# FFN down projection with two levels of seven products, the weight sums made by accumulating DMAs

## What is computed

```
h = _rmsnorm(x, norm_ffn_g[l]) * (1.0 + sc2) + sh2
y = (jax.nn.silu(h @ w_gate[l]) * (h @ w_up[l])) @ w_down[l]
x = x + g2 * y
...
return _rmsnorm(x, final_norm_g)
```

## Time and profile before

| | us |
|---|---|
| median of 3 runs | 3537.9 |
| lowest and highest | 3532.1, 3541.24 |
| span of the profiled execution (first to last instruction) | 3532.7 |
| PE busy in it | 3365.4 (95%) |
| DVE busy in it | 1703.2 (48%) |
| last product of the up projection ends | 3260.4 |
| passes 2, 4, 1, 3, 5, 7 of the down projection (L3409) | 226.6 |
| pass 6 (L3415) | 37.8 |
| from its end to the end of the span | 7.9 |

### The profile page before, as it was taken

How to read it: one execution, slowest core, us unless ns; L and a number is a source line. 1 busy time by engine, 2 the same in 40 slices (tenths; PEclk the granted TensorE clock), 3 DMA queues, 4 the chain that set the end, 5 groups by cost and what they waited for, 6 DMA issues and landing times. The chain is left out here.

```text
span 3532.7 us, 43811 instructions
## 1 busy us (share of the span) xinstructions
PE 3365.4 (95%) x17353; PEld 1781.7 (50%) x17353; DVE 1703.2 (48%) x2971; ACT 887.7 (25%) x1814; POOL 441.8 (13%) x329
## 2 busy tenths in 40 slices
PE   7999999899999899999979999898999999999999
PEld 4544444566555544444454577556654444444443
DVE  3579999766556400000124356555643434434336
ACT  2321111455332212111132122223543111111001
POOL 0033451222000011111201111111000000000000
PEclk8999999999999799999989999999999999999999
DMA  5213231222555699999952132213030111111434
GB/s 191 84 56 129 96 114 61 95 71 39 176 197 213 228 378 405 405 407 404 331 198 74 63 119 67 92 55 109 22 107 19 36 48 48 36 48 51 144 109 167
DMA packets 209426, 502.72 MB, mean 142 GB/s; under 512 B 22572, under 2 KB 93431, under 8 KB 195674
## 3 DMA queue, kind: packets, MB, share of 16 engines
q1 hardware_dynamic: 193090, 462.49, 35.9%
q0 software_dynamic: 10416, 30.14, 3.1%
q10 hardware_dynamic: 5736, 7.53, 0.6%
HBM read 447.90 MB, written 57.21 MB: 143 GB/s over the span
## 5 line engine op out<-in xcount | busy, mean ns | idle before, releaser
L600 PE MATMUL ch_side<-aT,space 128*128 128x512 f32 x896 | 393.2, 597 | 0.0
L1938 PE MATMUL jn_duo<-space,dsa 128*128 128x512 f32 (+1 forms) x736 | 328.4, 599 | 3.5 <-ACT dsa L2021 3.1
L600 PEld LDWEIGHTS ch_side<-aT,space 128*128 128x128 f32 x896 | 168.7, 191 | 213.0 <-issue 211.0
L3301 PE MATMUL en_bank<-en_h,en_up 128*128 128x512 f32 x528 | 233.8, 592 | 0.0
L1938 PEld LDWEIGHTS jn_duo<-space,dsa 128*128 128x128 f32 (+1 forms) x736 | 124.3, 173 | 151.6 <-issue 151.6
L2058 DVE TENSOR_TENSOR dsa<-dsa,jn_duo 128x512 f32<-128x512 f32 x24 | 16.5, 687 | 335.2 <-PE jn_duo L1938 335.2
L726 DVE MAX8 ch_best<-ch_score 128x8 f32<-128x384 f32 (+5 forms) x192 | 171.6, 894 | 6.1
L2452 PE MATMUL mx_duo<-mx_chunks,mx_region 128*128 128x512 f32 x384 | 172.3, 603 | 0.0
L727 DVE MATCH_REPLACE8 ch_score<-ch_best,ch_score 128x384 f32<-128x384 f32 (+5 forms) x192 | 168.0, 875 | 0.0
L3301 PEld LDWEIGHTS en_bank<-en_h,en_up 128*128 128x128 f32 x528 | 100.2, 190 | 125.8 <-issue 125.8
L3301 PE MATMUL en_bank<-en_h,en_mixed_up 128*128 128x512 f32 x352 | 158.2, 592 | 0.0
(11 more groups left out here) (596 smaller groups left out, 5643.9 us busy)
## 6 DMA issues: line engine op xcount, KB each, us to landing
space<-exp_w SPq DMA_DIRECT2D x62, 2048.0 KB, 21.6
aT<-exp_w SPq DMA_DIRECT2D x34, 2048.0 KB, 20.2
en_up<-w_down SPq DMA_DIRECT2D x132, 256.0 KB, 3.6
space<-ada_w SPq DMA_DIRECT2D x12, 2048.0 KB, 8.6
space<-w_ada SPq DMA_DIRECT2D x12, 2048.0 KB, 8.4
space<-proj_padded SPq DMA_DIRECT2D x96, 256.0 KB, 3.6
aT<-w_in SPq DMA_DIRECT2D x7, 2048.0 KB, 8.6
en_up<-w_gate SPq DMA_DIRECT2D x22, 512.0 KB, 4.6
```

The costliest lines, as they stand in the source:

```text
L600: last = nc.tensor.matmul(side_ps[i % 2][:, :], hT[:, k, t * P:(t + 1) * P], w[n % 2][:, k, :], start=k == 0, stop=k == KD - 1)
L1938: last = nc.tensor.matmul(ps[mine, :], xT[:, k, mine], up_view(ring[place])[:, k, :], start=k == 0, stop=k == KD - 1)
L3301: last = nc.tensor.matmul(to[:, :], a[:, k, :], b[:, k, :], start=k == 0, stop=k == HK - 1)
```

## The change

The down projection is cut a second time. FINE = 4, 1, 2, 5, 7, 6 are the six outer products that come first; each is now made by seven inner products again, on halves of 256 columns and 256 tokens. LAST = 3 is made as pass 6 was before, tile by tile.

- A fine step takes two slices of A and two of w_down (STARTS = 0, 2, 5, 7, 9; five steps) and makes the seven inner products, each of two matmuls of 128 tokens by 256 columns: 14 matmuls (L3446). Slice 4 is left over (ODD): `odd_step` does it plainly in eight matmuls of 256 columns. All eight banks are in use in every pass.
- `split` on DVE makes the inner sums for a fine step: two additions of 128x512 and four of 128x256, on A and on the weights in turn, two steps ahead of PE. `mix_act` sums the outer blocks of A in place, two slices at once. After each pass `post` adds the inner products into the four corners of the outer product (eight additions from PSUM) and ACT copies the first; `collect` and `settle` put the outer products together.
- The outer sums of w_down are no longer made on DVE. SP loads the first block of a sum into a ring of eight places of two slices (512 KB), and POOL issues DMAs that add the other blocks to it in memory (`accum_op`, L3597). TERMS gives the blocks: four for product 4, three for 6, two for 5 and 7, one for 1, 2 and 3. An addition waits until the one before it in the same place has landed. DVE, PE and ACT wait for the last one of the step.
- Two places of the ring and the third pair of split buffers are in rows 4 to 7 of `x3`. SP therefore stores these rows to x2 (four stores of 512 KB) once i = 20 has begun, and loads them again behind the last fine pass.

```
-            for n, (m, k, (j, half)) in enumerate(loads):
-                ...
-                sp.dma_start(raw[n % len(raw)], down_v[:, R * j + k, half * CH:(half + 1) * CH]).then_inc(raw_loaded[n % len(raw)], 16)
+            for t in range(HT, NT):
+                sp.dma_start(rows(g.d["x2"])[:, t, :], x3[:, t, :]).then_inc(lent_out, 16)
+            for s in range(len(all_steps)):
+                if s == 0:
+                    sp.wait_ge(lent_out, 16 * HT)
+                elif s == 2:
+                    sp.wait_ge(made, 7 * (G - 1))
+                elif s == 4:
+                    sp.wait_ge(made, 7 * (G - 1) + 2)
+                elif s == 6:
+                    sp.wait_ge(multiplied, 4 * R)
+                elif s >= len(b_ring):
+                    after_step(sp, user_before[s])
+                sp.dma_start(b_place(s), b_source(s, 0)).then_inc(b_loaded[entry_of[s]], 16)
...
+        FINE, LAST = (4, 1, 2, 5, 7, 6), 3
+        STARTS, ODD = (0, 2, 5, 7, 9), 4
+        TERMS = {1: ((0, 0),), 2: ((1, 0),), 3: ((1, 1),), 4: ((0, 0), (0, 1), (1, 1), (1, 0)), 5: ((0, 0), (0, 1)), 6: ((0, 0), (0, 1), (1, 1)), 7: ((0, 1), (1, 1))}
...
+                for j in (1, 6, 7, 5, 2, 4, 3):
+                    if i == 0:
+                        bank_free(n, j)
+                    ends = i == PAIRS - 1 and j in (1, 6, 7, 5)
+                    for t in range(2):
+                        last = nc.tensor.matmul(product_bank[j][:, t * QC:(t + 1) * QC], pairs[j][0][:, t * P:(t + 1) * P], pairs[j][1], start=i == 0 and t == 0, stop=ends and t == 1)
...
+        @block.gpsimd
+        def _(pool):
+            adds = ((s, n) for s, (m, i) in enumerate(all_steps) for n in range(1, len(TERMS[m])))
+            for s, n in adds:
+                if n == 1:
+                    pool.wait_ge(b_loaded[entry_of[s]], 16 * (len(uses_before(s)) + 1))
+                else:
+                    pool.wait_ge(b_added[entry_of[s]], 16 * (adds_before(s) + n - 1))
+                pool.dma_start(b_place(s), b_source(s, n), accum_op=ALU.add).then_inc(b_added[entry_of[s]], 16)
...
+            def split(n, i):
+                ...
+                TT(by_two_of(s31), by_two_of(a[:, 0, :]), a[:, :, high], ALU.subtract).then_inc(a_split, 1)
+                TT(by_two_of(t13), by_two_of(b[:, 0, :]), b[:, :, high], ALU.add).then_inc(b_split, 1)
+                dve.wait_ge(a_split, 3 * q + 1)
+                TT(s24[:, low], a[:, 0, low], s31[:, high], ALU.subtract).then_inc(a_split, 1)
+                dve.wait_ge(b_split, 3 * q + 1)
+                TT(t24[:, low], t13[:, low], b[:, 1, high], ALU.add).then_inc(b_split, 1)
+                dve.wait_ge(a_split, 3 * q + 2)
+                TT(s24[:, high], s24[:, low], a[:, 1, low], ALU.subtract).then_inc(a_split, 1)
+                dve.wait_ge(b_split, 3 * q + 2)
+                TT(t24[:, high], t24[:, low], b[:, 1, low], ALU.add).then_inc(b_split, 1)
...
+            for n, m in enumerate(FINE):
+                for i in range(PAIRS):
+                    fine_step(n, m, i)
+                odd_step(n, m)
```

More of the change, by code:

```diff
@@ new lines, in odd_step @@
+            def odd_step(n, m):
+                s = STEPS * n + PAIRS
+                act_ready(m, PAIRS)
+                wait_weights(pe, s)
+                pe.wait_ge(odd_turned, n + 1)
+                bank_free(n, 8)
+                a, b = act_part(*A_AT[m], ODD), b_ring[entry_of[s]]
+                for j, r, side in ((2, 0, b[:, 0, 0:QC]), (4, 1, b[:, 0, 0:QC]), (3, 0, b[:, 1, 0:QC]), (8, 1, b[:, 1, 0:QC])):
+                    for t in range(2):
+                        last = nc.tensor.matmul(product_bank[j][:, t * QC:(t + 1) * QC], a[:, (2 * r + t) * P:(2 * r + t + 1) * P], side, start=j == 8 and t == 0, stop=t == 1)
+                    last.then_inc(finished, 1)
@@ L3411, in _ @@
-            pe.wait_ge(gathered, 6 * HT)
-            for t in range(HT):
-                for k in range(R):
-                    a, b = operands(6, k)
-                    last = nc.tensor.matmul(low_bank(6, t)[:, :], a[:, t * P:(t + 1) * P], b, start=k == 0, stop=k == R - 1)
-                last.then_inc(lowered, 1)
+            for n, m in enumerate(FINE):
+                for i in range(PAIRS):
+                    fine_step(n, m, i)
+                odd_step(n, m)
+            pe.wait_ge(kept, len(FINE))
@@ new lines, in _ @@
+            for tiles in ((0, 1), (2,), (3,)):
+                for t in tiles:
+                    if t >= 1:
+                        pe.wait_ge(posted, 8 * (len(FINE) - 1) + (0, 1, 2, 4)[t])
+                for i in range(STEPS):
+                    s = N_FINE + i
+                    act_ready(LAST, i)
+                    wait_weights(pe, s)
+                    for r, k in enumerate((STARTS[i], STARTS[i] + 1) if i < PAIRS else (ODD,)):
+                        a = act_part(*A_AT[LAST], k)
+                        for t in tiles:
+                            last = nc.tensor.matmul(low_bank(t)[:, :], a[:, t * P:(t + 1) * P], b_ring[entry_of[s]][:, r, :], start=i == 0 and r == 0, stop=i == PAIRS)
+                            if i == PAIRS:
+                                last.then_inc(lowered, 1)
@@ L3619, in _ @@
                 else:
-                    for k in range(len(a_ring)):
-                        mix_step(2, k)
+                    split(0, 0)
+                    split(0, 1)
                 dve.wait_ge(made, 7 * i + 6)
@@ L3667, in finish @@
+            def finish(n):
+                t = ENDS[n]
+                dve.wait_ge(rooted, n + 1)
                 chain(nc.vector.reciprocal(last_stat[:, t:t + 1], last_stat[:, t:t + 1]))
[L3668 removed]
+                if n == 0:
                     dve.wait_ge(gain_loaded, 16)
[L3670 to L3680 removed]
@@ new lines, in _ @@
+            for what in ("21-6", "22-6", "12-6"):
+                for r in range(2):
+                    collect(len(FINE), what, r)
+            for r in range(2):
+                for j in range(2):
+                    settle(1, j, r, 0)
+                for j in range(2):
+                    settle(1, j, r, 1)
+                if r == 1:
+                    finish(0)
+                    finish(1)
+            for r in range(2):
+                settle(0, 1, r, 0)
+                settle(0, 1, r, 1)
+                finish(2 + r)
```

397 lines of the change are left out of this document (218 added, 179 removed).

## The result

The change made the kernel slower: 3546.3 us median of 10 runs (3539.5 to 3560.3), beside 3534.6 for the kernel before (10 runs, 3527.2 to 3541.2). The ratio is 1.0044, with a 95% interval of 1.0033 to 1.0054. The same kernel once more, later, beside other runs of before, gave 1.0040 (1.0025 to 1.0054). The forecast was 3518 with a range up to 3545, and both results lie above it; the mechanism is the one of rivals B and C.

The account below looks back on a forecast made before the run. PE was taken to bound the down projection: -24.4 us for fewer columns, +3.2 for a wait on POOL's additions, +1.0 for the clock, -20.2 in sum, from a median of 3537.9 to about 3518 us, range 3510 to 3545.

Parts of the forecast that it names:

- rival B: First fine pass, steps 2 to 5: slow additions decide; gain gone at L = 6.8; chance 0.15 with L over 7.6.
- rival C: POOL's chain, L from 6 to 7.6: the wait takes most of the gain, 3527 to 3548 us; chance 0.16.
- PE's price: Down projection: 256-column matmul 0.432 us, fine pass 33.7 instead of 37.8, stage 24.4 us less.
- DVE: Splits of 2.6 us, fullest pass product 6 with 29.4 beside PE's 33.7, about 27 in the last pass: stays hidden.
- T: Landing of the first weight load of product 4's chain, 35.1 us ahead of the down projection.
- the chain's period, 2L + i: POOL's additions for product 4: 11.0 us from step to step, with POOL's issue i = 0.6; 3.2 us of wait.
- L: Time from issue to landing of one 512 KB addition by POOL: 5.2 us, the middle of 4.8 and 5.5.
- a sentence that stood in brackets: POOL's chain for product 4: a step's third addition overlaps with the first of the next.
- the scatters' 12.7: Median landing in us of adding scatters into x_rows, under full load; upper bound for L, kept only in the chances.
- The break-even: First fine pass: the gain of 24.4 us is gone at L = 6.8.
- The clock: PE behind its wait in the first fine pass: restart at the 1.2 GHz level, 1.0 us added.
- The later passes: Fine passes after product 4: additions cost nothing until L passes 8; POOL spends 5.8 us on each product 6 step.

Follow-up runs that it names:

- the kernel with the early additions: Changed kernel with all eight rows of x3 lent earlier, so product 4's 18 additions run during the up projection: 3510.7 us, ratio 0.9942.
- the woven order: Changed kernel with product 4's 18 additions issued in turn across steps 0 and 1, then 2 to 5: 3512.2 us; once more, 3517.0 us.

## Why the prediction was wrong

**PE's price held.** A fine step of 6.05 us, an odd step of 3.45 and a pass of 33.7 are what the rows show, in every kernel. The 24.4 us were there to be had: PE works 240.1 us of the stage without the additions and 240.0 with the additions moved forward, where it was 264.5 before. The stage with its tail takes 22.6 and 23.2 less than before. The missing part is the tail, below.

**DVE held in the fine passes, and the sum missed it in the last.** A split takes 2.65 us (3313.96 to 3316.61), 2.6 were forecast; the fullest fine pass has 28.3 us of DVE (it is product 7's, not product 6's), 29.4 were forecast. In the last pass it was said to have 27 us of work and has 36.0 of 37.7. It did not delay PE, but work runs longer behind the last tile: the tail is 8.8 instead of 8.0 here, and 8.4 to 10.7 in the other profiles. The longest ones, 9.3 to 10.7, have the store of an earlier tile in their chain, where before it runs from PE's last matmul straight to the last tile's own work.

**T held.** The first load landed 34.8 us before the stage began; 35.1 was forecast.

**The step that failed is the chain's period, 2L + i = 11.0; it was 16.7.** Step 4 could begin 54.1 us after the start of the stage (3316.74 - 3262.6); the forecast said 27.4. The 26.7 between them are: T 0.3; four periods that were 5.7 longer each, 22.8; the three additions of step 4 itself with their issues, 19.1 for 15.6, 3.5; and 0.1 for the split. The 5.7 of a period have these parts. L was 6.0 instead of 5.2, which is 1.6 of them. Another 0.6 is the 0.29 us that POOL let pass between a landing and its next issue, twice a period, which the sum left out. The other 3.5 is nearly all a sentence that stood in brackets, that the third addition overlaps with the first of the next. They do overlap, but such a pair takes 10.0 us on the mean from the first issue to the second landing, and not L + i, which is 5.8, or 6.6 with the right L. In the forecast the overlap was taken as free; it cost twice what the wrong L did. With L = 6.0 alone, the forecast's own formula gives 13 us of wait, and about 2 for the clock: near 3529, inside the range and within 0.3% of no change. (The medians add a little: before was 3537.9 in three runs and 3534.6 in ten.) For the stage with its tail the forecast was 240.0 + 3.2 + 1.0 + 7.9 = 252.1 us, and 280.9 were measured. Of the 28.8 between them 22.1 are waits, 4.9 slow steps behind them, 0.3 the sixth pass and 0.9 the tail; the last 0.6 are ends of records, which overlap the next one where PE does not wait.

**Why the pair is slow.** An addition uses the engines for 3.2 us (the earlier trace rows had given 3.0) and waits some 3. A pair needs 6.4 us of engines, and loads of SP came on top: from 3241 to 3251 POOL's queue had 66.1% of the engines and SP's 35.7%, together full. Without the loads the second of a pair took 7.6 to 7.9 us instead of 9.5 to 10.6. The kernel with no loads beside the additions tells the two apart: its pairs are issued at 3252.14, 3267.73, 3282.43 and 3297.39, so a period is 15.1 us on the mean there (and 14.9 to 15.1 in the kernel with the early additions). So 4.1 of the 5.7 us of a period come without the loads, and 1.6 with them. The forecast said in rival B that the scatters' 12.7 was taken under a load that is not here; for the pairs it was here, because the loads of the ring fall into the same stretch.

**The break-even.** The forecast put it at L = 6.8, with rival B chiefly for L over 7.6. The measured L of a single addition is 6.0, on the side of faster; the time came out where rival C has it for L of 7.6. A range set by L alone could not hold the result for the right reason; what was missing was a second variable, the time of two in flight.

**The clock.** The sum had 1.0 us for one wait of 3.2. The three steps behind the waits took 2.4, 1.8 and 1.7 us longer than others, 5.9 together, at a granted clock of 0.50 in their first 3 us. Mechanism and size are nearly those of the earlier trace rows, 1.5 us behind a wait of 3.4; the waits were more and longer.

**The later passes** were to be untouched until L passes 8. That held for products 5 and 7, and narrowly not for 6: POOL needs 9.3 to 11.4 us for a step with two additions, not the 5.8 of one L + i. It is the same wrong overlap, seen a second time, worth 0.3 us in one profile and 3.1 plus a slow restart in another.

**What stays open.** From median to median the kernels differ by up to 5 us more or less than by their stages (the woven order: 3512 and 3517 with one and the same kernel). The stage's start moved by up to 8.7 us between profiles, all of it ahead of the up projection, where every kernel has the same work; what does that is not known. Where between landing, queue and read-modify-write the 3 us of latency of an addition lie can't be told from these rows.

## What to carry to other kernels

In a chain of dependent DMAs the price was that of the landing, not of the bytes alone; count for each link what else is in flight, and price a pair as a pair. If the links are independent between buffers, issue them across buffers rather than buffer by buffer: that alone was worth 25 us of the stage here, with not one transfer less. And sums that depend on nothing computed can be made long before they are wanted, if a place can be lent for them; delaying the other traffic instead only moved the collision.

## What the runs showed of the hardware

- A DMA of POOL that adds 512 KB from memory into SBUF lands in 5.6 to 6.1 us alone (once in 6.6), in up to 14.7 with others in flight; the same transfer as a plain copy in 4.4 to 4.7. For 256 KB the fastest addition took 3.8.
- The Trainium skill (DMA: Bandwidth & Descriptors, Anatomy of one DMA) gives 2.0 us + bytes / 436e3, an estimate of 3.2 us for 512 KB; in these runs the plain copy into SBUF took 1.2 to 1.5 us more, and the measurement decides.
- An addition of 512 KB uses the 16 engines 2.9 to 3.3 us; the plain copy, 25.9% of 97 us for 8.13 MB, 1.6 us.
- POOL spends 1.20 us on issuing one of 512 KB (0.86 for 256 KB), 0.72 (0.54) for the plain one; the earlier trace rows had 0.53 for a plain transfer of 512 KB, and the sum took 0.6.
- The length of a wait alone does not tell whether it costs the clock. Behind 1.95 us in the kernel with never two in flight the next 3 us ran at 0.68, behind 1.43 us in the woven order at 1.00. Two profiles have nearly the same wait at the same place of the sixth pass. In the second profile of the changed kernel (3.08 us) the stretch behind it ran at 0.66 and 0.77, in the second of the woven order (3.05 us) at 1.00, the level of 2.4 GHz; both were full before it (columns as in the earlier trace rows, the changed kernel first):

```profile
3489.00:3492.00 3.00, 2.98 (x9) 2.53 (x10) 3.00 (x3) 0.41 (x1) 0.00 (x0) 0.66 0.56 87
3492.00:3495.00 3.00, 3.00 (x12) 2.47 (x12) 3.00 (x4) 0.01 (x1) 0.00 (x0) 0.77 0.00 0
```

```profile
3455.40:3458.40 3.00, 3.00 (x14) 2.67 (x15) 3.00 (x3) 0.42 (x1) 0.00 (x0) 1.00 0.53 87
```

- Up to four additions in flight on different buffers kept POOL's queue at 82% of the engines; one or two at a time used 61% of them with no loads beside and 55% in the changed kernel.
